# One-hots of the first keys: from one VectorE instruction to four GpSimd instructions per step

## The chip, the cores and the metric

The kernel runs on one core of a Trainium2 chip. The metric is the device time of one launch in microseconds (us). The engines that matter here are TensorE (PE in the rows; PEld is its weight load), VectorE (DVE), ScalarE (ACT) and GpSimd (POOL). Each runs its own list of instructions in order, and they wait for each other through semaphores.

## What is computed

The reference is one inference step of a two-layer hybrid trunk on 640 tokens (128 context tokens, 512 latent tokens, width 1024). Each layer has a token mixer and then a PEER feed-forward: every token picks, for each of 8 heads, 16 out of 128 x 128 experts, and sums their outputs with softmax gates.

```python
sc = einsum('thpd,hpnd->thpn', q, subkeys)          # scores of 128 first and 128 second keys
sv, si = top_k(sc, 16)
cand = sv[:, :, 0, :, None] + sv[:, :, 1, None, :]
cidx = si[:, :, 0, :, None] * 128 + si[:, :, 1, None, :]
top_v, top_p = top_k(cand.reshape(t, 8, 256), 16)
experts = take_along_axis(cidx.reshape(t, 8, 256), top_p, -1)   # 128 experts of a token
gates = softmax(top_v)
...
act = gelu(einsum('cd,chkd->chk', x, u_tab[experts]))
out = einsum('chk,chkd->cd', gates * act, v_tab[experts])
```

## The kernel before

The two layers are a loop on every engine except GpSimd, whose list is written out twice. In the feed-forward the first two tiles of 128 tokens gather their experts' rows from memory with indirect DMAs that GpSimd issues (line 565). The other three tiles (`ND` = 3) multiply by all 16384 experts and weigh the result with a **gate matrix**, which holds for every token a 128 x 128 square: the gate of expert (first key, second key), and zero elsewhere.

The squares are made in the stage that the change touches, the gate matrix expansion. For each of the three tiles:

1. VectorE picks the 128 experts of every token (`pick`: maxima, indices, softmax) and writes first keys, second keys and gates to `idx`.
2. TensorE transposes `idx` into a bank of its accumulator memory (PSUM), and ScalarE copies it to `idxT` (line 1322): now a column holds the 128 choices of one token.
3. The tile's 128 tokens are expanded in 32 steps of four tokens, called quads. For each of the four tokens one needs two one-hot matrices of 128 choices x 128 keys: `ohA` compares the token's first keys with the row `iota` (0 to 127), `ohB` compares its second keys and multiplies by its gates. TensorE multiplies `ohB` by `ohA` (line 975) and gets the square of the token; ScalarE copies the four squares of a quad into `stg` (line 1335). After 16 quads a DMA on ScalarE's queue stores half a tile to `gate_matrix` in memory.

VectorE makes both one-hots of a quad: `ohA` of four tokens in one instruction of 512 columns (line 1851), `ohB` in four instructions of 128 columns (line 1854). `ohA` has four buffers (`u`), `ohB` two (`u % 2`). So VectorE waits, before quad n, until TensorE has finished quad n-2 (semaphore `quad_full`), and TensorE waits for `oh_ready` of its quad, and for ScalarE to have emptied the bank of quad n-4 (`quad_ready`). The next tile's `pick` writes over the buffers' memory, and waits for `tile_expanded`, which ScalarE raises when it has copied the last quad (line 1345).

GpSimd does nothing in this stage. It waits for `g_stored[0]`, which all three tiles' first halves have to raise, issues four gathers into `got_a`, waits for `g_stored[1]` (the second halves) and goes on. Its only computing work in the kernel is a subtraction of 128 x 2048 in the token mixer (line 542, 11 times in a layer).

The same stage thus runs six times in a launch: three tiles in each of two layers, 192 quads.

Of the kernel before, what the change touches and what calls it, by code (L numbers as in the profile page):

```python
# [34 lines left out]
P = 128  # L35
# [57 lines left out]
ND = NT - NS  # L93
TD = ND * P
D0 = NS * P
QUADS = P // 4
N_QUAD = ND * QUADS
# [24 lines left out]
def layer_at(l, per_layer, n):  # L122

    return l * per_layer + n


def trunk(nc, weights, u_rows, v_rows, consts, x_in, cond, bcol, rows, lnrows, cache_k, cache_v, x_wait,
          y, new_dk, new_dv, new_gk, new_gv, gate_matrix):
    ctx = ExitStack()
    with ctx:  # L130
        def sem(name):
            return ctx.enter_context(nc.semaphore(name))
# [75 lines left out]
        prob, t = at("prob", [2, 2, 640], tmp_at)  # L208
        wd, t = at("wd", [2, 640], t)
        pT, t = at("pT", [2, 2, 5, P], t)  # L210
        o = t
        mhi = [at("mhi0", [SLOT], z_at + 2560, F32R)[0], at("mhi1", [SLOT], ck_at, F32R)[0]]
        sg, t = at("sg", [2, T], tmp_at + 3840 + 2 * D)
        mtmp, t = at("mtmp", [T], t)
        oall, _ = at("oall", [NT, 512], z_at)
        mT, t = at("mT", [KC, T], k_at)
# [3 lines left out]
        lnr, t = at("lnr", [2, D], t)  # L220
        otmp, t = at("otmp", [2, 256], t)
# [16 lines left out]
        ohA, _ = at("ohA", [4, 4, P], o)  # L238
# [4 lines left out]
        pairs, t = at("pairs", [HEADS, PAIRS], cand_at)  # L243
        whole, t = at("whole", [11, P], t, U32)
# [14 lines left out]
        idxT, o = at("idxT", [3, P], o)  # L259
# [34 lines left out]
        iota = const[:, C_IOTA:C_IOTA + P]  # L294
# [87 lines left out]
        idxT_full = sem("idxT_full")  # L382
        idxT_ready = sem("idxT_ready")
        oh_ready = sem("oh_ready")
        quad_full = sem("quad_full")
        quad_ready = sem("quad_ready")
        tile_expanded = sem("tile_expanded")
# [135 lines left out]
        @block.gpsimd  # L523
        def _(pool):
            pool.dma_start(const[:, :], consts).then_inc(setup, 16)
            pool.dma_start(x[:, :, :], x_in.rearrange("t p d -> p t d")).then_inc(setup, 16)
            pool.dma_start(cnd[:, :, :], cond.rearrange("p (k s) -> p k s", s=2)).then_inc(setup, 16)
            for l in range(LAYERS):
                def one(ap):
                    return ap[l:l + 1]  # L530
                pool.wait_ge(layer_free, l + 1)
                pool.dma_start(bc[:, :], one(bcol).rearrange("o p n -> (o p) n")).then_inc(params, 16)
                pool.dma_start(row[:, :], one(rows).rearrange("o n -> (o n)").partition_broadcast(P)).then_inc(params, 16)
                pool.dma_start(ckb[:, :], one(cache_k).rearrange("o p n -> (o p) n")).then_inc(params, 16)
                pool.dma_start(V[:, 5, :], one(cache_v).rearrange("o p n -> (o p) n")).then_inc(params, 16)

                pool.dma_start(one(x_wait).rearrange("o t p d -> p (o t) d"), x[:, :, :]).then_inc(x_away, 16)

                for k in range(N_IN):
                    p = POSITION[IN_SLOT[k]]  # L540
                    pool.wait_ge(in_hi_ready, layer_at(l, N_IN, k + 1))
                    nc.gpsimd.tensor_tensor(ring_lo[:, p, :], ring[:, p, :], in_hi[k % 2][:, :].bitcast(F32),
                                            ALU.subtract).then_inc(in_lo_ready, 1)

                pool.wait_ge(blk_ready, layer_at(l, N_BLK, 2))
                pool.dma_start(one(new_gk).rearrange("o p n -> (o p) n"), zk[:, 0, :]).then_inc(kv_stored, 16)
                pool.wait_ge(z_ready, layer_at(l, N_Z, 5 * 9))
                pool.dma_start(one(new_dk).rearrange("o p n -> (o p) n"), z[:, 0, 0, :]).then_inc(kv_stored, 16)
                pool.dma_start(one(new_dv).rearrange("o p n -> (o p) n"), V[:, 0, 0:512]).then_inc(kv_stored, 16)
                pool.dma_start(one(new_gv).rearrange("o p n -> (o p) n"), V[:, 0, 512:640]).then_inc(kv_stored, 16)  # L550

                pool.wait_ge(row_full, layer_at(l, 2, 2))
                pool.dma_start(lnr[:, :, :], lnrows[l * 2:l * 2 + 1].rearrange("o a n -> (o a n)")  # L553
                               .partition_broadcast(P)).then_inc(ln1_rows, 16)

                pool.wait_ge(g_stored[0], layer_at(l, 16 * ND, 16 * ND))

                def gather(phase, k):

                    n = phase * P + k  # L560
                    if n == GB // 2:
                        pool.wait_ge(g_stored[1], layer_at(l, 16 * ND, 16 * ND))
                    if n >= GB:
                        pool.wait_ge(got_used, layer_at(l, N_GATHER, n - GB + 1))
                    pool.indirect_dma_start(  # L565
                        out=got[n % GB], out_offset=None,
                        in_=u_rows[:, :] if phase % 2 == 0 else v_rows[:, :],
                        in_offset=bass.IndirectOffsetOnAxis(ap=sidx[:, phase // 2, k:k + 1], axis=0),
                    ).then_inc(got_full[n % GB], 16)

                for phase in range(PHASES):
                    if phase % 2 == 0:
                        pool.wait_ge(sidx_ready, layer_at(l, NS, phase // 2 + 1))
                    for k in range(P):
                        gather(phase, k)
                pool.wait_ge(setup, 48)
                pool.wait_ge(v_full, layer_at(l, NB, NB))
                pool.dma_start(lnr2[:, :, :], lnrows[l * 2 + 1:l * 2 + 2].rearrange("o a n -> (o a n)")
                               .partition_broadcast(P)).then_inc(ln2_rows, 16)
            pool.wait_ge(kv_stored, 64 * LAYERS)  # L580
# [3 lines left out]
        def _(pe):  # L584
# [11 lines left out]
            with pe.Fori(0, LAYERS) as l:  # L596
# [250 lines left out]
                for pos, n in enumerate(BRANCHES):  # L847
# [9 lines left out]
                    for half in range(2):  # L857
                        slot = MERGE + 6 * pos + 3 * half
                        wb = ring[:, (slot + 1) % RING, :].rearrange("p (c n) -> p c n", c=4)
                        for dc in range(4):  # L860
# [19 lines left out]
                            for th in range(2):  # L880
                                ts = slice(th * TH, th * TH + TH)
                                src = [fT[:, c, ts] if n == 2 else brT[:, 4 * n + c, ts] for c in range(4)]
                                last = group(bank(b + th, 0, TH),
                                             [(wb[:, c, dc * P:dc * P + P], src[c]) for c in range(4)])
# [4 lines left out]
                for k in range(4):  # L889
# [3 lines left out]
                    for t in range(NT):  # L893
# [3 lines left out]
                        for c in range(KC):  # L897
                            if j == 0:
                                pe.wait_ge(mT_lo_ready, layer_at(l, KC, c + 1))
                            last = three(bank(j % 4, 0, 256), mT_hi[c][:, t * P:t * P + P], mT_lo[:, c, t * P:t * P + P],  # L900
                                         w_hi[:, c, :], w_lo[:, c, :], c == 0, c == KC - 1)
# [62 lines left out]
                def expand_tile(t, final=False):  # L964
                    pe.wait_ge(idx_ready, l * ND + t + 1)
                    for n in range(3):
                        last = turn(bank(4, n * P, n * P + P), idx[:, n, :])
                    last.then_inc(idxT_full, 1)
                    if not final:
                        score_tile(t + (NS + 1))  # L970

                    def quad(i, u):
                        pe.wait_ge(oh_ready, l * N_QUAD + t * QUADS + i * 4 + (u + 1))
                        for k in range(4):
                            last = mm(bank(4 + u, k * P, k * P + P), ohA[:, u, k, :], ohB[:, u % 2, k, :],  # L975
                                      start=True, stop=True)
                        last.then_inc(quad_full, 1)

                    for u in range(4):
                        quad(0, u)  # L980
                    with pe.Fori(1, P // 16) as i:
                        for u in range(4):
                            pe.wait_ge(quad_ready, l * N_QUAD + t * QUADS + i * 4 + (u - 3))
                            quad(i, u)
# [436 lines left out]
        def _(dve):  # L1421
# [14 lines left out]
            with dve.Fori(0, LAYERS) as l:  # L1436
# [407 lines left out]
                with dve.Fori(0, ND) as t:  # L1844
                    pick(t + NS, idx[:, 2, :], l * ND + t + 1).then_inc(idx_ready, 1)
                    dve.wait_ge(idxT_ready, l * ND + t + 1)

                    def onehots(i, u):

                        key = idxT[:, 0, bass.ds(i * 16 + 4 * u, 4)].unsqueeze(2).broadcast_to([P, 4, P])  # L1850
                        tt(ohA[:, u, :, :], iota.unsqueeze(1).broadcast_to([P, 4, P]), key, ALU.is_equal)
                        for k in range(4):
                            token = bass.ds(i * 16 + (4 * u + k), 1)
                            last = ts_(ohB[:, u % 2, k, :], iota, idxT[:, 1, token], idxT[:, 2, token], ALU.is_equal, ALU.mult)  # L1854
                        last.then_inc(oh_ready, 1)

                    for u in range(4):
                        if u >= 2:
                            dve.wait_ge(quad_full, l * N_QUAD + t * QUADS + (u - 1))
                        onehots(0, u)  # L1860
                    with dve.Fori(1, P // 16) as i:
                        for u in range(4):


                            dve.wait_ge(quad_full, l * N_QUAD + t * QUADS + i * 4 + (u - 1))
                            onehots(i, u)
# [241 lines left out]
```

## Time and profile before

| | us |
|---|---|
| median of 3 runs (lowest, highest) | 4756.47 (4753.83, 4761.77) |
| profiled execution, first to last instruction | 4758.8 |
| VectorE busy in it | 3480.5 |
| TensorE busy in it | 4085.3 |
| the six stretches of gate matrix expansion, together | 336.5 |

One profiled execution is read for durations; its own time is the span of 4758.8 us, 2.3 us above the median. A busy share is an average over stages with different limits, so the stage of the change is read by itself. In rows of the timeline the columns are start, length, engine, line, operation, tile written <- tiles read, shape, count, and in brackets the idle time of the engine before it and what ended that. Rows of the timeline that follow each other on an engine are merged, so that four instructions have one row.

### The profile page before, as it was taken

To read this page: it belongs to the slowest core of one execution; us is meant where nothing else is said; L and a number is where in the kernel's file an instruction comes from. 1 tells how busy PE (TensorE), PEld (TensorE's weight loads), DVE (VectorE), ACT (ScalarE), POOL (GpSimd) and SP (SyncE) were. 2 spreads that over 40 slices of the span, in tenths; PEclk is the share of its full clock that TensorE was granted. 3 is DMA by queue.
4 is the path that set the end of the run, shared out by engine and by line. 5 is a ranking of instruction groups with operands and counts; after the bars stand their busy time and mean duration, and the time that the engine had idled before them with its cause. 6 is when DMAs were issued, how large, how long until landed. Compare 5 with 4: busy or idle time off the path is not lost.

```text
span 4758.8 us, 66222 instructions
## 1 busy us (share of the span) xinstructions
PE 4085.3 (86%) x23702; PEld 3566.5 (75%) x23702; DVE 3480.5 (73%) x6376; ACT 1400.0 (29%) x1955; POOL 1807.3 (38%) x1075
## 2 busy tenths in 40 slices
PE   6889999833699999999887999997337999999996
PEld 5866888732599888988777678885236998889885
DVE  2417323889899999999952272248998999999998
ACT  2227211222323332333232361112223333323331
POOL 1100000000288777877622000000003887778774
PEclk9989999977899999999988999998779999999998
DMA  5320112313599999999853101123227999999996
GB/s 216 123 87 1 54 62 93 116 53 107 182 395 404 388 392 372 407 390 393 327 203 130 59 1 62 62 102 107 71 80 260 400 398 395 395 371 404 398 393 250
DMA packets 328016, 1083.15 MB, mean 228 GB/s; under 512 B 25632, under 2 KB 123984, under 8 KB 276112
## 3 DMA queue, kind: packets, MB, share of 16 engines
q0 software_dynamic: 151168, 552.73, 30.0%
q1 hardware_dynamic: 76688, 472.42, 25.4%
q10 hardware_dynamic: 99968, 55.58, 3.9%
q8 instruction: 104, 1.70, 0.1%
q14 instruction: 88, 0.72, 0.0%
HBM read 1021.11 MB, written 59.51 MB: 227 GB/s over the span
## 4 chain that ended last, share of the span: by engine, by line
PE 32%; DVE 32%; POOL 13%; DVEq 9%; issue 8%; DMA 5%; ACT 2%; ACTq 0%; SPq 0%; POOLq 0%
PE PS L590 9%; POOL got_a L565 6%; POOL got_b L565 6%; DVE acc L1903 6%; PE PS L599 5%; PE PS L600 5%; PE PS L601 5%; DVE ring_lo L1873 5%; DVE ohB L1854 3%; DVEq L1895 3%; DVE spare L1903 3%; DVEq L1880 2%; PE PS L594 2%; DMA ring<-weights 2%; PE PS L764 2%
## 5 line engine op out<-in xcount | busy, mean ns | idle before, releaser
L565 POOL DMA_INDIRECT got_a<-u_rows,sidx x256 | 433.9, 1695 | 1218.9 <-DMA gate_matrix<-stg 1121.5
L1313 ACT CAST ring_hi<-ring 128x2048 fp32r<-128x2048 f32 x256 | 489.7, 1914 | 1271.6 <-DMA ring<-weights 1271.6
L599 PE MATMUL PS<-hT_hi,ring_hi 128*128 128x384 f32 x2048 | 687.2, 336 | 12.8 <-DVE ring_lo L1873 12.8
L601 PE MATMUL PS<-hT_hi,ring_lo 128*128 128x384 f32 x2048 | 687.0, 335 | 0.0
L600 PE MATMUL PS<-hT_lo,ring_hi 128*128 128x384 f32 x2048 | 686.4, 335 | 0.0
L599 PE MATMUL PS<-ring_hi,W_hi 128*128 128x512 f32 x1536 | 608.6, 396 | 56.4 <-DVE W_lo L1889 56.4
L600 PE MATMUL PS<-ring_lo,W_hi 128*128 128x512 f32 x1536 | 605.6, 394 | 0.0
L601 PE MATMUL PS<-ring_hi,W_lo 128*128 128x512 f32 x1536 | 604.9, 394 | 0.0
L1873 DVE TENSOR_TENSOR ring_lo<-ring,ring_hi 128x2048 fp32r<-128x2048 f32 x256 | 585.0, 2286 | 0.0
L565 POOL DMA_INDIRECT got_b<-u_rows,sidx x256 | 443.0, 1730 | 138.9 <-issue 71.3
L565 POOL DMA_INDIRECT got_b<-v_rows,sidx x256 | 422.9, 1652 | 158.8 <-DVE acc L1903 88.7
L565 POOL DMA_INDIRECT got_a<-v_rows,sidx x256 | 390.1, 1524 | 120.2 <-issue 52.8
L599 PEld LDWEIGHTS PS<-hT_hi,ring_hi 128*128 128x128 f32 x2048 | 385.3, 188 | 18.8 <-DVE ring_lo L1873 14.0
L600 PEld LDWEIGHTS PS<-hT_lo,ring_hi 128*128 128x128 f32 x2048 | 385.4, 188 | 4.8
L599 PEld LDWEIGHTS PS<-ring_hi,W_hi 128*128 128x128 f32 x1536 | 292.2, 190 | 125.8 <-DVE W_lo L1889 55.6
L601 PEld LDWEIGHTS PS<-hT_hi,ring_lo 128*128 128x128 f32 x2048 | 385.4, 188 | 0.0
L601 PEld LDWEIGHTS PS<-ring_hi,W_lo 128*128 128x128 f32 x1536 | 292.0, 190 | 62.1
L600 PEld LDWEIGHTS PS<-ring_lo,W_hi 128*128 128x128 f32 x1536 | 292.4, 190 | 58.4
L1900 DVE SCALAR_TENSOR_TENSOR got_a<-got_a,hT 128x1024 f32<-128x1024 f32 x256 | 304.5, 1221 | 29.1 <-issue 14.9
L553 POOL DMA_DIRECT2D lnr<-lnrows x2 | 1.1, 544 | 848.0 <-PE PS L833 848.0
L1900 DVE SCALAR_TENSOR_TENSOR got_b<-got_b,hT 128x1024 f32<-128x1024 f32 x256 | 302.7, 1218 | 14.8 <-DMA got_b<-u_rows,sidx 14.8
L975 PE MATMUL PS<-ohB,ohA 128*128 128x128 f32 x1536 | 224.2, 291 | 93.2 <-DVE ohB L1854 90.0
(282 smaller groups left out, 8322.3 us busy)
## 6 DMA issues: line engine op xcount, KB each, us to landing
ring<-weights SPq DMA_DIRECT2D x400, 1024.0 KB, 7.8
G<-gate_matrix SPq DMA_DIRECT2D x128, 384.0 KB, 9.0
gate_matrix<-stg ACTq DMA_DIRECT2D x10, 4096.0 KB, 15.9
gate_matrix<-stg ACTq DMA_DIRECT2D x2, 3584.0 KB, 17.3
x_wait<-x POOLq DMA_DIRECT2D x2, 2560.0 KB, 23.4
x<-x_wait ACTq DMA_DIRECT2D x10, 512.0 KB, 11.3
lnr<-lnrows POOLq DMA_DIRECT2D x4, 1024.0 KB, 5.2
got_a<-u_rows,sidx POOLq DMA_INDIRECT x256, 9.3
```

The lines of the kernel that those rows point to most:

```text
L565: pool.indirect_dma_start(out=got[n % GB], out_offset=None, in_=u_rows[:, :] if phase % 2 == 0 else v_rows[:, :], in_offset=bass.IndirectO ...
L590: last = mm(out, a, b, start=(n == 0), stop=(n == len(pairs) - 1))
L599: mm(out, a_hi, b_hi, start=first, stop=False)
L600: mm(out, a_hi, b_lo, start=False, stop=False)
L601: return mm(out, a_lo, b_hi, start=False, stop=final)
L975: last = mm(bank(4 + u, k * P, k * P + P), ohA[:, u, k, :], ohB[:, u % 2, k, :], start=True, stop=True)
L1313: nc.scalar.copy(ring_hi[s][:, :], ring[:, s, :]).then_inc(hi_ready, 1)
L1854: last = ts_(ohB[:, u % 2, k, :], iota, idxT[:, 1, token], idxT[:, 2, token], ALU.is_equal, ALU.mult)
L1873: tt(ring_lo[:, s, :], ring[:, s, :], ring_hi[s][:, :].bitcast(F32), ALU.subtract).then_inc(split_ready, 1)
L1895: dve.drain()
L1900: stt(b3, b3, 1.0, hs, ALU.mult, ALU.mult, accum_out=pick16[:, c:c + 1]).then_inc(got_used, 1)
L1903: stt(sums[c % 4], b3, weight16[:, c:c + 1], sums[c % 4], ALU.mult, ALU.add).then_inc(got_used, 1)
```

## The change

GpSimd, which was idle there, now makes `ohA`: for each of the four tokens of a quad one comparison of `iota` with that token's column of `idxT` (`tensor_scalar`, 128 columns). VectorE makes `ohB` alone. A new semaphore `ohA_ready` counts GpSimd's quads, and TensorE waits for it as well as for `oh_ready`. GpSimd starts a tile on `idxT_ready` and, from the fifth quad on, waits until TensorE has finished the quad four before. Its part stands ahead of the wait for `g_stored[0]`.

```diff
@@ semaphores
+        ohA_ready = sem("ohA_ready")
@@ GpSimd, in each layer, ahead of the gathers
+                def first_keys(t, q):
+                    if q >= 4:
+                        pool.wait_ge(quad_full, layer_at(l, N_QUAD, t * QUADS + q - 3))
+                    for k in range(4):
+                        last = nc.gpsimd.tensor_scalar(ohA[:, q % 4, k, :], iota, idxT[:, 0, 4 * q + k:4 * q + k + 1], None,
+                                                       ALU.is_equal)
+                    last.then_inc(ohA_ready, 1)
+
+                for t in range(ND):
+                    pool.wait_ge(idxT_ready, layer_at(l, ND, t + 1))
+                    for q in range(QUADS):
+                        first_keys(t, q)
 
                 pool.wait_ge(g_stored[0], layer_at(l, 16 * ND, 16 * ND))
@@ TensorE, quad(i, u)
+                        pe.wait_ge(ohA_ready, l * N_QUAD + t * QUADS + i * 4 + (u + 1))
                         pe.wait_ge(oh_ready, l * N_QUAD + t * QUADS + i * 4 + (u + 1))
@@ VectorE, onehots(i, u)
-                        key = idxT[:, 0, bass.ds(i * 16 + 4 * u, 4)].unsqueeze(2).broadcast_to([P, 4, P])
-                        tt(ohA[:, u, :, :], iota.unsqueeze(1).broadcast_to([P, 4, P]), key, ALU.is_equal)
                         for k in range(4):
                             token = bass.ds(i * 16 + (4 * u + k), 1)
                             last = ts_(ohB[:, u % 2, k, :], iota, idxT[:, 1, token], idxT[:, 2, token], ALU.is_equal, ALU.mult)
```

VectorE's list at the start of a tile, before (`const` holds `iota`; the last row of `pick` comes first):

```order
L1834 TENSOR_TENSOR idx<-pw,pm 128x128
L1851 TENSOR_TENSOR ohA<-const,idxT 128x512 [waits idxT_ready]
L1854 TENSOR_SCALAR ohB<-const,idxT 128x128 x4
L1851 TENSOR_TENSOR ohA<-const,idxT 128x512
L1854 TENSOR_SCALAR ohB<-const,idxT 128x128 x4
L1859 ISA
L1851 TENSOR_TENSOR ohA<-const,idxT 128x512 [waits quad_full]
```

The same place in VectorE's list of the change:

```order
L1851 TENSOR_TENSOR idx<-pw,pm 128x128
L1869 TENSOR_SCALAR ohB<-const,idxT 128x128 [waits idxT_ready]
L1869 TENSOR_SCALAR ohB<-const,idxT 128x128 x7
L1874 ISA
L1869 TENSOR_SCALAR ohB<-const,idxT 128x128 [waits quad_full]
```

The 512-column instruction of every quad is gone from VectorE; the four of 128 columns stand behind each other as before, and the wait for `quad_full` falls to the first of them.

GpSimd's list ahead of the gathers, before:

```order
L550 DMA new_gv<-V 128x128
L553 DMA lnr<-lnrows 128x2048 [waits row_full]
L565 DMA got_a<-u_rows,sidx 128x1024 [waits sidx_ready,g_stored0]
L565 DMA got_a<-u_rows,sidx 128x1024 x3
L565 DMA got_b<-u_rows,sidx 128x1024 [waits g_stored1]
```

The same place in GpSimd's list of the change; the pattern of its fifth and sixth rows repeats up to the gathers, which are now line 581:

```order
L551 DMA new_gv<-V 128x128
L554 DMA lnr<-lnrows 128x2048 [waits row_full]
L563 TENSOR_SCALAR ohA<-const,idxT 128x128 [waits idxT_ready]
L563 TENSOR_SCALAR ohA<-const,idxT 128x128 x15
L563 TENSOR_SCALAR ohA<-const,idxT 128x128 [waits quad_full]
L563 TENSOR_SCALAR ohA<-const,idxT 128x128 x3
...
L581 DMA got_a<-u_rows,sidx 128x1024 [waits sidx_ready,g_stored0]
L581 DMA got_a<-u_rows,sidx 128x1024 x3
L581 DMA got_b<-u_rows,sidx 128x1024 [waits g_stored1]
```

In each layer 384 comparisons (3 tiles x 32 quads x 4) now stand ahead of the first gather, with a wait for each quad from the fifth of a tile on.

## Rows read from the trace of the kernel before

**Rows 1.** The page: span, busy time and instructions of each engine.

```profile
span 4758.8 us, 66222 instructions
PE 4085.3 (86%) x23702; PEld 3566.5 (75%) x23702; DVE 3480.5 (73%) x6376; ACT 1400.0 (29%) x1955; POOL 1807.3 (38%) x1075
```

**Rows 2.** Windows: first tile of layer one (us; busy and count of each engine); sum over six tiles.

```profile
1011.00:1066.50 55.50, 40.03 (x288) 34.00 (x286) 52.27 (x160) 18.98 (x33) 0.00 (x0) 0.97 0.26 76
...
sum 336.50, PE 234.91 PEld 198.86 DVE 318.75 ACT 126.34 POOL 9.05; mean PE 39.15 PEld 33.14 DVE 53.13 ACT 21.06 POOL 1.51
```

**Rows 3.** Waits in the first tile, 1011 to 1066.5 us: total, times, longest.

```profile
PE PS L975 <- DVE ohB L1854: 14.5, 30, 0.9
```

**Rows 4.** By source line: duration ns min/median/max, first and last start us.

```profile
L1851 DVE TENSOR_TENSOR ohA<-const,idxT x192: 674/686/694, 1011.3 to 3614.4; 128x512 f32<-128x512 f32 x192
L1854 DVE TENSOR_SCALAR ohB<-const,idxT x768: 329/343/515, 1011.9 to 3615.8; 128x128 f32<-128x128 f32 x192
```

**Rows 5.** Timeline: one step in the middle of the first tile.

```profile
1024.17 1.11 DVE L1854 TENSOR_SCALAR ohB<-const,idxT 128x128 f32<-128x128 f32 x4
...
1025.19 0.68 DVE L1851 TENSOR_TENSOR ohA<-const,idxT 128x512 f32<-128x512 f32 x1
...
1025.33 1.16 PE L975 MATMUL PS<-ohB,ohA 128*128 128x128 f32 x8 [0.47 <-DVE ohB L1854]
1025.80 1.10 DVE L1854 TENSOR_SCALAR ohB<-const,idxT 128x128 f32<-128x128 f32 x4
1026.61 0.58 ACT L1335 COPY stg<-PS 128x512 f32 x1 [1.04 <-PE PS L975]
```

**Rows 6.** Timeline: first tile's end, and VectorE's start on the next pick.

```profile
1063.23 1.12 DVE L1854 TENSOR_SCALAR ohB<-const,idxT 128x128 f32<-128x128 f32 x4
1066.55 0.30 DVE L1752 MAX8 sv<-PS 128x8 f32<-128x128 f32 x1 [2.21 <-issue]
...
1070.45 0.09 DVE L1759 MATCH_VALUE_LOAD work<-sv,PS 128x8 f32 x1 [0.30 <-issue]
...
1067.02 0.19 ACT L1345 COPY lamw<-const 128x1 f32<-128x1 f32 x1 [0.75 <-ACT stg L1335]
```

**Rows 7.** GpSimd's computing instructions: line 542, and its shortest (count, busy us, mean ns).

```profile
L542 POOL TENSOR_TENSOR ring_lo<-ring,in_hi x22: 4488/4611/5482, 54.9 to 2615.3; 128x2048 fp32r<-128x2048 f32 x22
...
L2101 POOL MEMSET const-float32-0.0<- 128x1 f32 x1 | 0.1, 98 | 0.3 <-issue 0.3
```

**Rows 8.** Timeline: VectorE starts beside a running GpSimd instruction; then line 1468's durations.

```profile
54.95 4.49 POOL L542 TENSOR_TENSOR ring_lo<-ring,in_hi 128x2048 fp32r<-128x2048 f32 x1 [38.08 <-ACT in_hi L1092]
...
56.69 3.30 DVE L1468 TENSOR_SCALAR xn<-x,mv,rstd 128x1024 f32<-128x1024 f32 x1
...
L1468 DVE TENSOR_SCALAR xn<-x,mv,rstd x18: 800/807/3302, 56.7 to 3230.2; 128x1024 f32<-128x1024 f32 x18
```

**Rows 9.** Timeline: GpSimd starts beside a running VectorE instruction.

```profile
162.31 1.23 DVE L1534 TENSOR_TENSOR z<-rot 128x1024 f32<-128x1024 f32 x1
162.54 5.37 POOL L542 TENSOR_TENSOR ring_lo<-ring,in_hi 128x2048 fp32r<-128x2048 f32 x1 [5.72 <-ACT in_hi L1092]
```

**Rows 10.** Timeline: end of the third tile and the first gathers; landing time last.

```profile
1251.97 1.00 POOL L565 DMA_INDIRECT got_a<-u_rows,sidx  x1 [560.80 <-DMA gate_matrix<-stg]
1253.28 0.97 POOL L565 DMA_INDIRECT got_a<-u_rows,sidx  x1 [0.30 <-issue]
...
1260.94 1.16 PE L975 MATMUL PS<-ohB,ohA 128*128 128x128 f32 x8 [0.47 <-DVE ohB L1854]
...
1268.48 1.21 DVE L1900 SCALAR_TENSOR_TENSOR got_a<-got_a,hT 128x1024 f32<-128x1024 f32 x1
...
1277.13 0.96 DVE L1883 TENSOR_TENSOR wtmp<-act_g,G 128x768 f32<-128x768 f32 x1 [6.29 <-ACT act_g L1377]
...
1280.80 2.60 POOL L565 DMA_INDIRECT got_b<-u_rows,sidx  x1 [23.39 <-DMA gate_matrix<-stg]
...
got_a<-u_rows,sidx POOLq DMA_INDIRECT x256, 9.3
```

## The prediction

> **What bounds the kernel now.** The page comes first, and here it misleads: TensorE is busy 86% of the span, VectorE 73% [rows 1]. Those are averages over stages with different limits, so I read the stage of the change alone, by windows. In the gate matrix expansion VectorE works 52.27 of 55.5 us, TensorE 40.03 and GpSimd nothing; over all six tiles VectorE works 318.75 of 336.5 us [rows 2]. The waits say the same from the other side: TensorE waits for `ohB` 30 times in a tile [rows 3], once for nearly every one of its 32 quads.
>
> The timeline shows the period. `ohB` of one quad starts at 1024.17 and of the next at 1025.80 [rows 5], so a quad takes 1.63 us: about 0.61 for `ohA` (which starts at 1025.19 and lets `ohB` start at 1025.80) and 1.02 for the four `ohB`. TensorE's four products, eight records, take 1.16 us and ScalarE's copy 0.58, both beside it. VectorE's list is the limit, and 192 quads of 1.63 us are 313 us. Nothing beside the stage hides its length, since the next pick, and after the third tile the feed-forward's main loop, wait for it. Each 0.1 us on a quad is 19.2 us on the kernel.
>
> **What is taken away.** 192 `ohA` instructions of 686 ns leave VectorE [rows 4]; they cost 0.61 us of the period each, as the next instruction starts before the end of the record. If nothing took their place, VectorE could go at 1.02 us a quad, but `ohB` has only two buffers. A buffer's round is four `ohB` (1.11 us), 0.05 us to the matmul's start, the products (1.16) and 0.12 us until the waiting engine starts (1025.33 + 1.16 = 1026.49; ScalarE starts at 1026.61) [rows 5]. That is 2.44 us for two quads. The floor is therefore 1.22 us a quad, 0.41 below now: at most 0.41 x 192 = 79 us to gain.
>
> **What is added.** 768 GpSimd instructions, four in a quad. GpSimd has four `ohA` buffers and may run ahead, so its own rate counts. Call x the time from one comparison to the next: GpSimd allows a quad every 4x. Up to 0.30 us it is hidden behind the floor; at 0.407 (1.63 / 4) everything gained is given back; above it the kernel is slower.
>
> No row of before has such a comparison, so I bound x. From below there are the shortest GpSimd instructions, 98 ns for one column [rows 7]; a comparison near that price is hidden. The nearest row in kind is line 542, 2048 columns in 4.49 to 4.61 us [rows 7]. Its time has two parts. At 162.54 it starts while a VectorE instruction that reads two tiles runs on to 163.54; it is 1.00 us late in reaching the data, yet takes only 0.76 us longer than its usual 4.61 [rows 9]. So some 0.24 us of it is preparation that can go beside VectorE. The rest, about 4.37 us, is 2.13 ns a column, or 0.27 us for 128 columns. Together x = 0.24 + 0.27 = 0.51 us.
>
> Line 542 reads two tiles and a comparison reads one, which speaks for less; a comparison must also fetch a scalar for each partition, which speaks for more. I keep 0.51.
>
> **The port.** The trace shows that the two engines stop each other. At 56.69 VectorE starts a `tensor_scalar` on 1024 columns while line 542 runs; it ends at 59.99, 0.55 us after line 542 does (59.44), and takes 3.30 us where 0.80 is usual [rows 8]. It was held until GpSimd had finished, with its first 0.25 us already done. `ohB` is the same instruction on 128 columns: 343 ns against 800 for 1024 [rows 4, 8] give 0.51 ns a column, which is 0.065 us of data and 0.28 of fixed time. If the two take turns, VectorE's 0.065 us of data fall into GpSimd's 0.24 us of preparation, and VectorE's fixed time into GpSimd's 0.27 us of data. Then the port costs nothing beyond x, and a quad takes 4 x 0.51 = 2.04 us. If nothing overlaps, a comparison costs 0.51 and an `ohB` its 0.256 (1.02 / 4), and a quad takes 3.06. These are my two ends above; I take the lower, as rows 8 and 9 both show preparation done while the other engine held the data.
>
> The Trainium skill has the rule on this: "SBUF — State Buffer", section "Who interferes with whom", says that VectorE and GpSimd share one pair of ports, that it is an exclusive lock, held for a whole instruction, and that `tensor_scalar` can be of the kind that takes it. By that the sum would be the upper end, 3.06 us a quad, if nothing overlapped. Rows 8 agree that the later one blocks.
>
> **Smaller terms.** TensorE's second wait stands in front of the four products, and the copy to `stg` waits behind them; a semaphore that is already up costs at most the 0.05 us seen ahead of the matmul, and it is inside the 1.63 as much as inside the 2.04, so I set nothing. The end of a tile gains a little. Now VectorE's last `ohB` ends at 1064.35, the next pick begins 2.2 us later, and its first write over the buffers comes at 1070.45, though `tile_expanded` is up by 1067.21 [rows 6]. In the change VectorE's last quad waits only for TensorE's quad two before, so it ends some 2.5 us ahead of TensorE, not 1.2; the pick can start 1.3 us earlier. Four tiles have a pick behind them: 5 us less.
>
> The gathers move. Today the first starts at 1251.97, before the third tile ends; in the change it stands behind the last comparison, which ends about 1.3 us before TensorE does (1262.10), so at some 1260.8 on today's clock. With 9.3 us to land the first row is there at 1270.1, 1.6 us after VectorE takes it today (1268.48), and the second 1.3 us later. VectorE then stands idle for 6.29 us until 1277.13 [rows 10], which hides both. The gathers into `got_b` wait for `g_stored[1]` until 1280.80 anyway. Price zero, and up to 1.6 us in each layer if that idle time were gone.
>
> **The sum.** (2.04 - 1.63) x 192 = 79 us more, 5 less: 4758.8 + 74 = 4833 for the profiled execution, and since its span is 2.3 us above the median, 4830.
>
> **The rivals.**
>
> *A GpSimd comparison is cheap.* With one tile to read, the data part could be half (0.14 us) and the preparation hidden by the comparison before it. The point that decides is x = 0.407. At x = 0.35 a quad takes 1.40, and the kernel 44 us less, 4712; at 0.30 and below it stands at the floor, 79 us less, 4677. For it speaks that 98 ns is enough for a small GpSimd instruction [rows 7]; against it the 0.24 us of preparation [rows 9]. Chance 0.28. The Trainium skill's "GPSIMD Engine Reference", section "4.1 Engine selection", speaks for this rival, as it calls GpSimd's one-input work roughly line-rate; no run here shows that.
>
> *The engines take the port in turns with nothing overlapped.* Each instruction holds it from start to end. A quad takes 3.06 us, 1.43 more: 275 us, 5028 after the small terms. For it speaks the 3.30 us of rows 8, against it the 0.25 and 0.24 us done beside the other. Chance 0.17.
>
> *Nothing to be measured.* x between 0.395 and 0.42 puts the time within 0.2% (9.5 us), about what a measurement of this kernel can tell from no change. Chance 0.07.
>
> *The forecast:* x from 0.42 to 0.65 us with what is left of the port's waits, 4765 to 4945. Chance 0.48.
>
> **How the numbers follow.** The predicted time is that of the likeliest, 4830. Slower by over 0.2% is the forecast and the second rival, 0.65; the same 0.07; faster 0.28. The forecast alone would need 4765 to 4945. For 8 in 10 the range goes down to 4700, which leaves out the third of the first rival that is nearest the floor (0.10), and up to 4990, which leaves out the part of the second above it (0.10).
>
> **What would show it.** In the changed kernel GpSimd should be busy through the six tiles, TensorE should wait for `ohA` instead of `ohB`, and `ohB` starts should be 2.0 us apart for each four. Some `ohB` records should be well above 343 ns, since they wait for the port. The `pick` stretches should keep their length. I am wrong if GpSimd's comparisons stand under 0.40 us apart, if TensorE still waits for `ohB`, or if a quad takes over 2.6 us with comparisons that are themselves short, which would be the port.

## The result

The change makes the kernel slower: 4901.81 us median (4896.82 to 4908.72, 4 runs) against 4755.15 us of the kernel before, a ratio of 1.0305 with a 95% interval of 1.029 to 1.0319, or 147 us. The prediction was 4830 us, slower, in a range of 4700 to 4990. The profiled execution spans 4899.3 us, 140.5 more than before. The loss is about twice the predicted one of 74 us, and lies inside the range.

The page of the changed kernel, its first lines and its row for the new instructions:

```profile
span 4899.3 us, 66864 instructions
PE 4178.5 (85%) x23702; PEld 3647.4 (74%) x23702; DVE 3400.5 (69%) x6184; ACT 1401.0 (29%) x1955; POOL 2282.1 (47%) x1843
...
L563 POOL TENSOR_SCALAR ohA<-const,idxT 128x128 f32<-128x128 f32 x768 | 463.2, 628 | 811.7 <-ACT idxT L1339 811.7
```

Beside [rows 1] VectorE has lost 80 us of work and GpSimd has gained 475; no share on this page says which of the two matters. The windows of the six tiles do (the first and the third tile of layer one, and the sum):

```profile
1009.00:1088.00 79.00, 56.62 (x290) 48.45 (x288) 41.57 (x140) 19.23 (x33) 74.68 (x128) 0.72 0.18 54
...
1246.00:1331.00 85.00, 55.57 (x256) 47.67 (x256) 46.71 (x131) 24.81 (x36) 84.14 (x131) 0.68 0.18 52
...
sum 486.00, PE 338.89 PEld 290.56 DVE 258.23 ACT 127.07 POOL 467.47; mean PE 56.48 PEld 48.43 DVE 43.04 ACT 21.18 POOL 77.91
```

The stretches have grown from 336.5 [rows 2] to 486 us, by 149.5 us, but these windows are rounded, and those of the change reach a little past the tiles. From the end of the copy to `idxT` to the end of the last copy to `stg` the six tiles took 332.8 us before and take 479.8 now, 147.0 more. That is more than the span has grown, since the four stretches between the tiles became 6.7 us shorter. The whole loss is in this stage. GpSimd is now busy in 467 us of the windows where VectorE was in 319. The waits in the first tile, where [rows 3] had TensorE waiting for `ohB`:

```profile
DVE ohB L1869 <- PE PS L992: 33.6, 28, 2.0
...
PE PS L992 <- POOL ohA L563: 21.1, 31, 1.2
```

TensorE waits for GpSimd's `ohA` 31 times in 32 quads, and VectorE, which was the limit, now waits for TensorE. The durations by source line, where [rows 4] had 686 ns for `ohA` of a whole quad:

```profile
L563 POOL TENSOR_SCALAR ohA<-const,idxT x768: 592/604/4516, 1010.0 to 3745.6; 128x128 f32<-128x128 f32 x192
...
L1869 DVE TENSOR_SCALAR ohB<-const,idxT x768: 332/346/554, 1009.9 to 3741.7; 128x128 f32<-128x128 f32 x192
```

A comparison on GpSimd takes 604 ns at the median, `ohB` 346 (343 before). One step of the timeline, for [rows 5]:

```profile
1038.69 7.57 POOL L563 TENSOR_SCALAR ohA<-const,idxT 128x128 f32<-128x128 f32 x13
...
1040.52 2.07 PE L992 MATMUL PS<-ohB,ohA 128*128 128x128 f32 x8 [1.17 <-POOL ohA L563]
...
1042.78 1.26 DVE L1869 TENSOR_SCALAR ohB<-const,idxT 128x128 f32<-128x128 f32 x4 [1.90 <-PE PS L992]
1042.84 2.08 PE L992 MATMUL PS<-ohB,ohA 128*128 128x128 f32 x8 [0.24 <-POOL ohA L563]
1045.04 0.59 ACT L1352 COPY stg<-PS 128x512 f32 x1 [1.73 <-PE PS L992]
```

The 13 comparisons in one row show GpSimd going without a pause, (7.57 - 0.60) / 12 = 0.58 us from start to start. Products start 2.32 us apart (1040.52, 1042.84), where a quad of [rows 5] took 1.63. The whole tile gives the mean: GpSimd's 128 comparisons fill 74.68 us, 0.583 each, 2.33 a quad.

The end of the third tile holds what the prediction had not seen. The timelines of GpSimd, TensorE and VectorE there, engine by engine:

```profile
1319.22 4.37 POOL L563 TENSOR_SCALAR ohA<-const,idxT 128x128 f32<-128x128 f32 x2
1323.57 4.52 POOL L563 TENSOR_SCALAR ohA<-const,idxT 128x128 f32<-128x128 f32 x1
1328.13 2.07 PE L992 MATMUL PS<-ohB,ohA 128*128 128x128 f32 x8 [7.46 <-POOL ohA L563]
...
1319.85 3.34 DVE L1883 TENSOR_TENSOR hT_lo<-hT,hT_hi 128x3072 fp32r<-128x3072 f32 x1
1323.12 4.57 DVE L1888 TENSOR_TENSOR ring_lo<-ring,ring_hi 128x2048 fp32r<-128x2048 f32 x2
...
1346.67 0.96 DVE L1898 TENSOR_TENSOR wtmp<-act_g,G 128x768 f32<-128x768 f32 x1 [10.05 <-DMA G<-gate_matrix]
```

VectorE has made its last `ohB` and goes on to the main loop's first subtractions, which read two tiles each, while GpSimd still has two comparisons to do. The first row merges two: a usual comparison (0.62 us from 1319.22), and one of 3.79 us that starts at 1319.80 and ends at 1323.59, 0.39 us after the subtraction beside it (1323.19). The next takes 4.52 us and ends at 1328.08, 0.39 us after the second `ring_lo` (1327.69). TensorE waits 7.46 us for it, the half tile is stored late, and VectorE then waits 10.05 us for `G`.

### The profile page after: what moved, and what is told of

Read it like the earlier page. It is cut to its first block, busy times and chain, and to the rows that moved or that the text cites. A ratio compares the mean times of both kernels' runs of the same rounds, so it can differ in the third digit from the quotient of the medians.

```text
span 4899.3 us, 66864 instructions
## 1 busy us (share of the span) xinstructions
PE 4178.5 (85%) x23702; PEld 3647.4 (74%) x23702; DVE 3400.5 (69%) x6184; ACT 1401.0 (29%) x1955; POOL 2282.1 (47%) x1843
## 4 chain that ended last, share of the span: by engine, by line
PE 30%; DVE 26%; POOL 22%; DVEq 8%; issue 7%; DMA 5%; ACT 2%; ACTq 0%; SPq 0%; POOLq 0%
POOL ohA L563 9%; PE PS L606 9%; POOL got_a L581 7%; POOL got_b L581 6%; DVE acc L1918 6%; PE PS L615 5%; PE PS L616 5%; PE PS L617 5%; DVE ring_lo L1888 4%; DVEq L1910 3%; DVE spare L1918 2%; DMA ring<-weights 2%; DVEq L1895 2%; PE PS L610 2%; PE PS L780 2%
## 5 line engine op out<-in xcount | busy, mean ns | idle before, releaser
L563 POOL TENSOR_SCALAR ohA<-const,idxT 128x128 f32<-128x128 f32 x768 | 463.2, 628 | 811.7 <-ACT idxT L1339 811.7
L581 POOL DMA_INDIRECT got_a<-u_rows,sidx x256 | 455.3, 1779 | 93.2 <-issue 75.0
L581 POOL DMA_INDIRECT got_b<-u_rows,sidx x256 | 427.3, 1669 | 128.8 <-issue 72.5
L992 PE MATMUL PS<-ohB,ohA 128*128 128x128 f32 x1536 | 323.3, 376 | 140.9 <-POOL ohA L563 140.9
L992 PEld LDWEIGHTS PS<-ohB,ohA 128*128 128x128 f32 x1536 | 276.7, 271 | 187.4 <-POOL ohA L563 186.6
L1869 DVE TENSOR_SCALAR ohB<-const,idxT 128x128 f32<-128x128 f32 x768 | 234.8, 371 | 215.9 <-PE PS L992 205.5
```

What stands on the lines that cost most here:

```text
L563: last = nc.gpsimd.tensor_scalar(ohA[:, q % 4, k, :], iota, idxT[:, 0, 4 * q + k:4 * q + k + 1], None, ALU.is_equal)
L581: pool.indirect_dma_start(out=got[n % GB], out_offset=None, in_=u_rows[:, :] if phase % 2 == 0 else v_rows[:, :], in_offset=bass.IndirectO ...
```

## The experiments

The theory: a comparison costs GpSimd 0.58 us by itself, which sets the pace, and VectorE's subtractions behind the third tile hold the last two. Its rival: the comparison is shorter (the prediction had 0.51 us or less) and the rest is waiting for the port that VectorE's `ohB` holds.

### One `ohB` in a quad

```diff
-                        for k in range(4):
+                        for k in range(3, 4):
                             token = bass.ds(i * 16 + (4 * u + k), 1)
 ...
-  ohA[:, u, k, :], ohB[:, u % 2, k, :],
+  ohA[:, u, k, :], ohB[:, u % 2, 3, :],
```

> VectorE makes one ohB of a quad instead of four (the fourth, which all four products of the quad then use; three quarters of the second one-hots and gates are left out). Theory A, a GpSimd comparison costs 0.58 us by itself: the starts of comparisons stay 0.577 to 0.58 us apart, a quad takes 2.31 us, the time stays within 4885 to 4905 us. Theory B, the comparison is short and waits for the port that ohB holds: with a quarter of the ohB the distance falls to 0.45 to 0.51 us, a quad to 1.8 to 2.05 us, the time to 4780 to 4850 us.

Measured: 4902.0 us (one run). The comparisons of this kernel by source line:

```profile
L563 POOL TENSOR_SCALAR ohA<-const,idxT x768: 590/597/4581, 1012.6 to 3746.1; 128x128 f32<-128x128 f32 x192
```

With a quarter of the `ohB` a comparison takes 597 ns instead of 604. So `ohB`'s use of the port is not what makes it long. The rival falls here, and the maximum of 4581 ns at the third tile's end stays, as it should: those subtractions are still there.

### Every `ohB` twice

```diff
                             token = bass.ds(i * 16 + (4 * u + k), 1)
+                            ts_(dup[:, u % 2, k, :], iota, idxT[:, 1, token], idxT[:, 2, token], ALU.is_equal, ALU.mult)
                             last = ts_(ohB[:, u % 2, k, :], iota, idxT[:, 1, token], idxT[:, 2, token], ALU.is_equal, ALU.mult)
```

> VectorE makes every ohB twice, the first copy into memory that nobody reads: eight instructions in a quad, 8 x 0.256 = 2.05 us of its time, still under the 2.31 us that GpSimd needs. Theory A, the port costs nothing while the two engines take turns: the distance of the comparisons stays at 0.58 to 0.60 us and the time within 4895 to 4935 us. Theory B, each ohB holds GpSimd up: a quad grows by four times 0.07 to 0.26 us, 0.26 to 1.0 us, the time to 4950 to 5095 us.

Measured: 4893.7 us (one run). The comparisons and VectorE's two groups (count, busy us, mean ns, idle before):

```profile
L564 POOL TENSOR_SCALAR ohA<-const,idxT x768: 592/599/693, 1008.6 to 3740.9; 128x128 f32<-128x128 f32 x192
...
L1870 DVE TENSOR_SCALAR dup<-const,idxT 128x128 f32<-128x128 f32 x768 | 297.5, 387 | 13.5 <-ACT idxT L1340 9.0 <-PE PS L993 1.2
L1871 DVE TENSOR_SCALAR ohB<-const,idxT 128x128 f32<-128x128 f32 x768 | 264.7, 345 | 0.0
```

Twice the `ohB` leave a comparison at 599 ns, and GpSimd still waits for nothing inside a tile. In steady work GpSimd loses nothing to the port; VectorE pays, with 44 ns on every other instruction (387 against 343). It has no time left: a quad takes 2.33 to 2.35 us, where eight times 0.256 is 2.05, and VectorE's waits for TensorE in this stage have gone from 205.5 us to 1.2. It goes in step with GpSimd, two instructions beside each comparison, and in the first tile most of TensorE's waits (24 of 31) are for `ohB` again.

This single run is about 8 us faster than the median of the change. The maximum shows a cause: no comparison is over 693 ns, and the third tiles take 77.6 and 77.7 us instead of 84.9 and 85.2. VectorE, with twice the work, is no longer early at the third tile's end: its first subtraction starts at 1320.52, as GpSimd's last comparison ends (1320.51).

### GpSimd's instructions by themselves

A row of instructions ahead of the first subtraction of the token mixer, in layer one, while GpSimd waits there; in `ts_` the third argument is the key. The 512-column comparisons run four times, the others eight.

```diff
+                    key = const[:, C_ID + 5:C_ID + 6]
+                    ts_ = nc.gpsimd.tensor_scalar
+                    for n in range(8):
+                        ts_(bench[:, n * P:n * P + P], iota, key, None, ALU.is_equal)
 ...
+                        ts_(bench[:, 1024 + n * 64:1024 + n * 64 + 64], iota[:, 0:64], key, None, ALU.is_equal)
 ...
+                        ts_(bench[:, 1536 + n * 512:1536 + n * 512 + 512], const[:, 0:512], key, None, ALU.is_equal)
 ...
+                        ts_(bench[:, 3584 + n * P:3584 + n * P + P], iota, 5.0, None, ALU.is_equal)
 ...
+                        nc.gpsimd.tensor_tensor(bench[:, 4608 + n * P:4608 + n * P + P], iota, const[:, 0:P], ALU.subtract)
```

> The kernel of the change with a row of GpSimd instructions added near its start, where GpSimd waits from 17 to 55 us and VectorE runs statistics that were not held up by GpSimd: 8 comparisons of 128 columns with a key from memory, 8 of 64, 4 of 512, 8 of 128 with a constant key, 8 subtractions of 128 columns that read two tiles. Theory A, the price is the comparison's own: 0.55 to 0.60 us from start to start for 128 columns. Theory B, it is the port: 0.40 to 0.50 us. Of the parts: if 0.21 us is preparation and the rest grows with the columns, 64 columns take 0.39 us and 512 take 1.7; if the key's fetch is part of it, the constant key takes 0.08 us or more less. The prediction's way from the subtraction's price, 0.24 + 0.27 = 0.51 us, is right if the 128-column subtraction takes 0.5 us. The time changes by under 10 us.

Measured: 4906.9 us (one run). GpSimd's timeline, one row for each group:

```profile
16.99 4.69 POOL L546 TENSOR_SCALAR bench<-const 128x128 f32<-128x128 f32 x8
21.67 3.32 POOL L548 TENSOR_SCALAR bench<-const 128x64 f32<-128x64 f32 x8
24.97 6.17 POOL L550 TENSOR_SCALAR bench<-const 128x512 f32<-128x512 f32 x4
31.21 4.67 POOL L552 TENSOR_SCALAR bench<-const 128x128 f32<-128x128 f32 x8
35.94 3.36 POOL L554 TENSOR_TENSOR bench<-const 128x128 f32<-128x128 f32 x8
```

From each group's start to the next, divided by its count: 0.585 us for a comparison of 128 columns, 0.41 for 64, 0.59 for 128 with a constant key. By their length (6.17 / 4 and 3.36 / 8) it is 1.54 for 512 columns, under the 1.7 expected, and 0.42 for the subtraction, under the 0.51 of the prediction's way. VectorE did nothing after 20.91 us until the row was over, so all groups but the first ran without it. Alone, a comparison costs what it costs in the kernel, so the price is its own. Its parts: (1.54 - 0.585) / 384 = 2.5 ns a column, and 0.585 - 128 x 2.5 = 0.26 us fixed. The key from memory costs nothing. The subtraction, which reads two tiles, is the cheaper of the two at 128 columns. With 4.49 us for 2048 [rows 8] it takes (4.49 - 0.42) / 1920 = 2.1 ns a column, and 0.42 - 0.27 = 0.15 us fixed.

### A wait ahead of VectorE's subtractions

```diff
+                dve.wait_ge(ohA_ready, l * N_QUAD + N_QUAD)
                 dve.wait_ge(hhi_ready, l + 1)
                 tt(hT_lo[:, :, D0:T], hT[:, :, D0:T], hT_hi[:, :, :].bitcast(F32), ALU.subtract).then_inc(hlo_ready, 1)
```

> One wait added on VectorE: before the subtraction for hT_lo, behind the last ohB of the third tile, it waits until GpSimd has finished the layer's last comparison. Theory A, that subtraction and the two for ring_lo behind it hold GpSimd's last two comparisons (3.79 and 4.52 us in the profile after, where 0.60 is usual): both go back to 0.60 us, the last quad's products start some 7.2 us earlier, VectorE's three subtractions start about 1 us later, and each layer gains 4 to 7 us: 4888 to 4895 us. Theory B, those two records are long for another reason: the time stays at 4902 us or grows by up to 4 us.

Measured: 4888.97 us (4883.96 to 4892.44, 4 runs), 1.0285 of the kernel before, interval 1.0268 to 1.0302. The comparisons by line, and the third tile's end in its timeline:

```profile
L563 POOL TENSOR_SCALAR ohA<-const,idxT x768: 590/596/721, 1011.0 to 3737.3; 128x128 f32<-128x128 f32 x192
...
1321.31 3.36 DVE L1884 TENSOR_TENSOR hT_lo<-hT,hT_hi 128x3072 fp32r<-128x3072 f32 x1 [2.23 <-POOL ohA L563]
1321.33 2.07 PE L992 MATMUL PS<-ohB,ohA 128*128 128x128 f32 x8 [1.15 <-POOL ohA L563]
...
1337.95 0.96 DVE L1899 TENSOR_TENSOR wtmp<-act_g,G 128x768 f32<-128x768 f32 x1 [0.75 <-ACT act_g L1394]
```

The long comparisons are gone (maximum 721 ns), VectorE waits 2.23 us and TensorE's last products start at 1321.33 instead of 1328.13. The wait of 10.05 us for `G` is gone as well. The medians differ by 13 us; the intervals of the two ratios overlap a little, so the size is known less well than the two traces show the cause.

### The work shared

Three kernels with the same added wait, in which GpSimd compares two, three or one of a quad's four tokens and VectorE the others in one instruction; the edit of the first:

```diff
-                    for k in range(4):
+                    for k in range(2):
                         last = nc.gpsimd.tensor_scalar(ohA[:, q % 4, k, :], ...
 ...
+                        key = idxT[:, 0, bass.ds(i * 16 + (4 * u + 2), 2)].unsqueeze(2).broadcast_to([P, 2, P])
+                        tt(ohA[:, u, 2:4, :], iota.unsqueeze(1).broadcast_to([P, 2, P]), key, ALU.is_equal)
```

> The work shared: GpSimd compares two of a quad's four tokens, VectorE makes the other two in one instruction of 256 columns beside its four ohB; with the wait for GpSimd's last comparison ahead of hT_lo. GpSimd then needs 2 x 0.58 = 1.16 us a quad, VectorE 0.34 + 1.02 = 1.37. Theory A, the port costs at most the 0.07 us by which ohB records that meet a comparison are longer, twice a quad: 1.37 to 1.51 us a quad, 0.12 to 0.26 below the kernel before, 4700 to 4730 us, faster than both kernels. Theory B, each comparison holds VectorE up for the 0.37 us in which it moves data, less VectorE's own fixed time: 1.57 to 1.75 us a quad, 4740 to 4780 us, no gain.

> GpSimd compares three tokens of a quad, VectorE one (128 columns), same added wait. GpSimd needs 3 x 0.58 = 1.74 us, VectorE 0.21 + 1.02 = 1.23. Theory A, GpSimd's own price sets the quad: 1.74 to 1.77 us, 0.12 above the kernel before, 4770 to 4780 us. Theory B, the port adds its waits: 1.9 to 2.1 us, 4800 to 4845 us.

> GpSimd compares one token of a quad (0.58 us), VectorE three (384 columns, 0.48 us) beside its four ohB, same added wait: VectorE sets the quad at 1.50 us if the port is free, a gain of 0.13 us: 4730 us; with one wait of 0.07 to 0.37 us for a comparison, 1.57 to 1.87 us: 4740 to 4800 us.

| GpSimd's tokens | us, median | ratio to before | interval |
|---|---|---|---|
| 1 | 4746.64 (10 runs) | 0.9976 | 0.9966 to 0.9985 |
| 2 | 4739.15 (5 runs) | 0.9956 | 0.9942 to 0.9969 |
| 3 | 4788.89 (4 runs) | 1.0062 | 1.0046 to 1.0077 |

The kernel before had 4758.6 us on the chip of these three. Groups of the kernel with two each, then of that with one (busy us, mean ns, idle before):

```profile
L563 POOL TENSOR_SCALAR ohA<-const,idxT 128x128 f32<-128x128 f32 x384 | 269.5, 717 | 840.0 <-ACT idxT L1339 830.8 <-PE PS L992 5.7
L1868 DVE TENSOR_TENSOR ohA<-const,idxT 128x256 f32<-128x256 f32 x192 | 81.7, 425 | 22.5 <-PE PS L992 11.9 <-ACT idxT L1339 9.0
L1871 DVE TENSOR_SCALAR ohB<-const,idxT 128x128 f32<-128x128 f32 x768 | 224.4, 354 | 0.0
```

```profile
L563 POOL TENSOR_SCALAR ohA<-const,idxT 128x128 f32<-128x128 f32 x192 | 185.4, 968 | 931.2 <-ACT idxT L1339 831.7 <-PE PS L992 99.5
```

With two each VectorE is the limit again (22.5 us idle in six tiles ahead of its `ohA`, none ahead of `ohB`), and its quad is shorter than before: a tile, by the same ends as above, takes 50.7 to 52.4 us instead of 55.0 to 55.8. This version beats the kernel before by a clear interval, though a small one. At 4739 us it lies between the two theories' ranges (to 4730, and from 4740), and neither is borne out whole: in the middle of a tile a quad takes 1.47 us in the first two tiles of a layer, as the first theory says, but 1.56 in the third (1.63 and 1.67 before). `ohB` is 11 ns longer at the mean than before, and comparisons that meet VectorE's instruction of two inputs take 828 ns at the mean, the others 600; GpSimd has the slack to pay for that. With one token the same holds: 1008 against 603 ns, and a quad of 1.51 us, the price with a free port, but 1.63 to 1.68 in the third tiles. So the kernel came out at 4747 us, in the range for a port that is not free; why the third tiles are slower is not shown. With three, GpSimd sets the pace: a tile takes 59.3 to 59.5 us, 3.5 to 4.4 above before, where 0.12 x 32 = 3.8 was expected. Its median is 9 us above the expected range; the six tiles add only 23, and the rest lies outside the stage, in stretches that differ by some us from run to run.

## Why the prediction was right, and where it was short

**The place and the sign held.** The time lies in the forecast's 4765 to 4945 us because x, at 0.583 us, lies in its 0.42 to 0.65; the size of the loss came out at half. VectorE was the limit at 1.63 us a quad, the change took 0.61 of that away, and GpSimd became the limit in its place: TensorE's waits changed from `ohB` to `ohA`, as the prediction asked for, and the experiments with a quarter of the `ohB` and with GpSimd alone show that it is GpSimd's own pace. Some `ohB` records are longer, as it said (371 ns at the mean, up to 554). Not all of that need be the port: the run with one `ohB` in a quad, each behind a wait, has 407 at the mean. The floor of 1.22 us was never reached.

**The term that was too small is x, the price of a comparison.** The prediction had 0.24 us of preparation and 0.27 us of data, 0.51 together. The 0.24 agrees with the comparison's 0.26 us by luck: both terms were taken from a subtraction, whose own fixed part in a row of instructions is 0.15, so that it costs 0.42 us for 128 columns and not 0.51. Its data term, 2.13 ns a column, was read rightly (2.1); the comparison takes 2.5, or 0.32 us for 128 columns. The step that fell short is taking the price of one operation for that of another. The prediction held "reads one tile, which speaks for less" against "must fetch a scalar, which speaks for more"; the runs show both wrong: a comparison is dearer for a column than a subtraction that reads two tiles, and the scalar is free. Whether the comparing or the form of the instruction makes the difference was not tested. At 2.33 us a quad the stage costs (2.33 - 1.63) x 192 = 134 us instead of 79.

**One term was missing.** [rows 9] showed that a VectorE instruction that reads two tiles stops GpSimd, and the prediction used it for the middle of a tile alone. It did not ask what VectorE does once it runs ahead of GpSimd. At the end of the third tile that is a 3072-column subtraction and two of 2048, and they hold two comparisons. From the end of the copy to `idxT` to the last copy to `stg` the third tiles took 84.9 and 85.2 us, the others 76.7 to 77.8; with the added wait the third took 77.7 and 77.8. That is some 15 us in the two layers; the added wait took 14.6 off these tiles, and 13 off the median.

**The small terms.** The next pick starts earlier, as was worked out: in the four stretches between tiles the profiled execution is 1.7, 2.6, 0.7 and 1.7 us shorter, 6.7 in all, where 5 was predicted. The later gathers cost what idle time hides, though barely: with the wait added, VectorE waits 0.75 us for `act_g` at 1337.95 instead of the 6.29 of [rows 10]. Sum: 134 + 15 - 7 = 142 us, against 140.5 in the profiled span and 147 between the medians; the difference between these two is within the spread of the runs.

**The rivals.** A cheap comparison fell: 0.585 us alone, above the deciding 0.407. Nothing overlapped at the port fell too, with 3.06 us a quad against 2.33: doubling VectorE's instructions left a comparison at 599 ns. The Trainium skill's "SBUF — State Buffer", section "Who interferes with whom", says that the one that issues first has the ports for its whole instruction and the other blocks. The trace agrees that one blocks: a comparison beside a long subtraction ends 0.39 us after it. As far as the records' starts tell, it does not bear out that the first goes first: the comparison held first starts at 1319.80, before the subtraction (1319.85), and the next one, from 1323.57, was passed by a subtraction that starts at 1325.42. In the middle of a tile, where VectorE's instructions are short, GpSimd loses nothing and VectorE pays; how the two take turns there no run shows. The other page of the Trainium skill, "GPSIMD Engine Reference", section "4.1 Engine selection", calls one-input work roughly line-rate, which would be 0.11 us for 128 columns at the 1.2 GHz of its section "1. Specifications", an estimate from that page. The comparison's 0.32 us differs, and the measurement decides.

## What to carry to other kernels

Work moved from the limiting engine to an idle one sets a new limit at its own price, so the break-even price comes first (here 0.407 us for a comparison that costs 0.58), and a share of the work that leaves both engines under the old limit can gain where the whole of it loses: two tokens of four gave 0.44%. Price an operation on GpSimd by the same operation at two sizes, not by another one with more inputs. When two engines can stop each other, look at what the faster one does next when it runs ahead, not only at the pair of instructions that the change puts side by side.

## What was not expected of the hardware

- GpSimd's comparison with one tile to read takes 2.5 ns a column and its subtraction with two takes 2.1; a key from memory (0.585 us) costs no more than a constant (0.59). Why the comparison is dearer is not shown.
- Two VectorE subtractions one behind the other can hold a GpSimd instruction through both: the comparison that started at 1323.57, after the first `ring_lo` had started at 1323.12, did not get its turn between them and ended 0.39 us after the second. In the run with the added row of instructions one comparison was held by all three subtractions and took 8.27 us. It is not always so: the comparison of 3.79 us did get its turn between two of them, and line 542 of [rows 9] ended at 167.91, ahead of the VectorE instruction that had started behind the first at 163.45 and took 5.55 us. What decides is not shown.
- TensorE's granted clock was 0.66 to 0.74 in the six windows of the change (its two levels are 1.2 and 2.4 GHz) where the first window of before had 0.97 [rows 2], while TensorE waited for GpSimd in nearly every quad; the products of 121 of the 192 quads then took over 1.5 us, up to 2.08, instead of 1.16. GpSimd waited for nothing inside a tile, so this cost nothing there, and up to 0.9 us at its end.
